# Where sixteen or seventeen pieces of context work stand among the expert products of a routed mixture

## The chip, the core and the metric

The kernel runs on one core of a Trainium2 chip. The metric is the device time of one execution in microseconds (us), lower is better. All data are fp32.

## What is computed

The reference is two residual blocks over 256 tokens of width 1024 (`x`), with 256 context tokens beside them (`ctx`). The part that matters here is the end of the first block and the start of the second:

```python
def hier_moe(h, wg, bg, we, be, w_gate, w_up, w_down):      # 4 groups of 8 experts, width 512
    p_group = softmax(t @ wg + bg);      g_idx = top 1 of 4 groups
    e_logits = (t @ we + be) of that group;  e_idx = top 2 of its 8 experts
    for gi in range(N_GROUPS):
        hid = silu(t @ w_gate[gi]) * (t @ w_up[gi]) * combine[:, gi]
        out = out + hid @ w_down[gi]

def second_block(x, c, ctx, ...):        # layer 0
    hc = rmsnorm(ctx, g_pre) * (1 + scale_c) + shift_c
    uc = hc @ w_in                        # q, k, v, gates, o, z, pool input and gate
    ... convolution, chunkwise mLSTM of 4 heads, head norm, multiscale pool, @ w_out
    ctx = ctx + gate_c * rmsnorm(yc, g_post)
```

The experts work on `x`, the second block's context side works on `ctx` alone, so the two are independent of each other. The kernel runs them in one stage.

## The kernel before, in words

The program is a list of stages. Each stage has one function for PE, one for ACT and one for DVE, and the engines meet at its end (`stage_end`). The stage of this case is the **expert stage**, `moe_pe`, `moe_act`, `moe_dve` and `moe_sync` (about 523 to 1167 us of the span). If no expert got too many tokens, it takes the sparse path: `sparse_pe`, `sparse_act`, `sparse_dve`, `sparse_sync`.

**The expert side.** The 32 experts are taken in 10 passes (`PASSES`): six passes of four experts, then four passes of two. Before a pass `gather(p)` (L2333) picks the tokens of the experts of that pass with one-hot products, and ACT and DVE copy them from two banks to `gath` (L2394, L2431). A pass has six **steps**, numbered 0 to 59 over all passes: two for the gate weights and two for the up weights (`project`, L2347), two for the down weights (`down`, L2364). Behind the fourth step stand the gather of the next pass, then four transposes of the hidden rows (L2380), which need DVE's product (L2453). A step of a four-expert pass reads four half-slots of 1 MB of weights, one of a two-expert pass reads two. There are 8 half-slots. SP issues the loads in order (L2219), and the load for half-slot number `at` waits until the step that used number `at - 8` has signalled `step_used`. So in a four-expert pass the weights of step n+2 are asked for when step n ends, and at most two steps of weights are on their way or waiting. In a two-expert pass it is four steps.

**The context side.** `body_pe`, `body_act` and `body_dve` are Python generators that emit the context work of the second block in 116 **pieces**, in a fixed order, with the same numbers on the three engines:

| pieces | work on PE | length on PE |
|---|---|---|
| 1 to 8 | keys and values of heads 0, 1 (L1418, L1433) | long, 3.5 us |
| 9 | gate columns (L1446, L1452) | 2.6 us |
| 10 to 27 | mLSTM heads 0 and 1: each one opening piece (L1463 to L1475), then eight small ones (L1486, L1491, L1497) | small, 0.7 to 2.7 us |
| 28 to 35 | output and gate rows (L1433) | long |
| 36 | transposes of the heads (L1506) | 1.2 us |
| 37 to 48 | queries, keys, values of heads 2, 3 | long |
| 49 to 66 | mLSTM heads 2 and 3 | small |
| 67 to 74, 75 | output and gate rows, transposes | long, 1.2 us |
| 76 to 83, 84 | pool input (L1418), an empty piece | long, 0 |
| 85 to 88 | pool products (L1522), each needs DVE's pool mean (L1900 to L1905), which needs the table `pool_inv` from DRAM | 2.0 us |
| 89 to 96 | pool gate (L1418) | long |
| 97 to 112 | output product (L1533, L1538) | long, 3.6 us |
| 113 to 116 | two norms | small, in a chain with ACT and DVE |

The context weights come through four slots of 1 MB that ACT loads (L1380), two of them when a projection has been taken from its banks. The pool tables are asked for at piece 79.

**How they are mixed.** `fill(body, p, i)` emits some pieces at the place i of pass p: places 0, 1, 2 behind the first three steps, 3 behind the fourth step and the gather, 4 behind the transposes, 5 behind the fifth step, 6, 7 and 8 behind the sixth, ahead of the first step of the next pass. In a four-expert pass the numbers are `FILL_FOUR`, in a two-expert pass `FILL_TWO`. `start(body)` emits four pieces between the first gather and the first pass, `finish(body)` emits what is left behind the last pass. ACT and DVE call the same functions at the same places of their own order, so that no engine waits for a piece that another one has not yet come to. On DVE `row_ids_dve` (L2301 to L2314, 16 small instructions) stands in pass 0 between the places 3 and 4. Behind `finish` ACT scales and DVE adds the experts' rows (L2426, L2477), which GpSimd has fetched back from DRAM (L2322).

Of the kernel before, what the change touches and what calls it, by code (L numbers as in the profile page):

```python
# [227 lines left out]
def build(nc, d, out):  # L228
    ctx = ExitStack()
    with ctx:  # L230
# [1989 lines left out]

        step_of = [n for n in range(6 * NPASS) for _ in range(PASSES[n // 6][1])]

        FILL_FOUR, FILL_TWO = (2, 2, 2, 2, 2, 2, 2, 1, 1), (0, 0, 0, 1, 0, 1, 0, 0, 0)

        def fill(body, p, i):

            for _ in range((FILL_FOUR if PASSES[p][1] == 4 else FILL_TWO)[i]):
                next(body, None)

        def start(body):  # L2230

            for _ in range(4):
                next(body, None)

        def finish(body):
# [89 lines left out]
        def sparse_pe(pe, body):  # L2325
            def gather(p):

                pe.wait_ge(pick_ready, p + 1)
                if p >= 2:
                    pe.wait_ge(py_out, 2 * p - 2)  # L2330
                for k in range(DT):
                    for t in range(TT):
                        mm = nc.tensor.matmul(bank[2 + k // 4][:, (k % 4) * P:(k % 4 + 1) * P], hrows[:, t, k * P:(k + 1) * P], pick[:, t, :],  # L2333
                                              start=(t == 0), stop=(t == 1), skip_group_check=True)
                    if k % 4 == 3:
                        mm.then_inc(gath_mm, 1)

            def project(p, b, n, at):

                experts = PASSES[p][1]  # L2340
                w = P // experts
                for half in range(2):
                    pe.wait_ge(step_in[(n + half) % 4], filled_to[n + half])
                    for k in range(4 * half, 4 * half + 4):
                        for e in range(experts):
                            rows = slice(e * w, (e + 1) * w)
                            mm = nc.tensor.matmul(bank[b][rows, :], gath[:, k, rows], half_slot[(load_at[n + half] + e) % NHALF][:, (k % 4) * 512:(k % 4 + 1) * 512],  # L2347
                                                  start=(k == 0), stop=(k == DT - 1), skip_group_check=True)
                    mm.then_inc(step_used, 1)
                    if at + half < 3:  # L2350
                        fill(body, p, at + half)
# [15 lines left out]
                    fill(body, p, 5 + half)  # L2367

            gather(0)
            start(body)  # L2370
            for p in range(NPASS):
                pe.wait_ge(gath_out, 2 * p + 2)
                project(p, 0, 6 * p, 0)
# [17 lines left out]
        def sparse_act(act, body):  # L2391
            def take_gathered(p):
                act.wait_ge(gath_mm, 2 * p + 1)
                nc.scalar.copy(gath[:, 0:4, :].rearrange("p k s -> p (k s)"), bank[2][:]).then_inc(gath_out, 1)  # L2394

            take_gathered(0)
            start(body)
            for p in range(NPASS):
                fill(body, p, 0)
                act.wait_ge(step_used, 6 * p + 2)  # L2400
# [27 lines left out]
        def sparse_dve(dve, body, chain):  # L2428
# [10 lines left out]
            def make_pick(p):  # L2439
                o, shape, first, experts, w = slots(p, pick)  # L2440
                nc.vector.tensor_tensor(o, bc(slot_no[:, 0:w].unsqueeze(1).unsqueeze(1), shape), bc(place[:, :, first:first + experts].unsqueeze(3), shape),  # L2441
                                        ALU.is_equal).then_inc(pick_ready, 1)

            make_pick(0)
            take_gathered(0)
            make_pick(1)
            start(body)
            for p in range(NPASS):
                for i in (0, 1, 2):
                    fill(body, p, i)  # L2450
# [790 lines left out]
```

## Time and profile before

| | |
|---|---|
| median of 3 runs | 1720.27 us (1718.19 to 1720.31) |
| the profiled execution | 1717.13 us, its span 1715.3 us |
| mean granted TensorE clock over the span | 0.944 |
| PE busy, DMA | 91% of the span; 397.57 MB, mean 232 GB/s |
| expert weights | 192 loads of 1 MB (SP), in three groups of 64 |
| context weights in this stage | 28 + 8 loads of 1 MB and the pool tables (ACT) |

PE is the matmul engine, PEld its weight loads, SPq and ACTq the queues that issue DMAs. The idle time in square brackets of a row is that of the engine just before the row, with what released it. A matmul in fp32 shows as two records.

### The profile page before, as it was taken

What the parts mean: (1) busy time and instruction counts of PE and PEld (TensorE: products, weight loads), DVE (VectorE), ACT (ScalarE), POOL (GpSimd) and SP (SyncE); (2) the same over time, 40 slices, a digit from 0 to 9 for tenths busy, and PEclk for the clock granted to TensorE, in tenths of its full rate; (3) what the DMA queues carried; (4) which work ended last, traced back from release to release, by engine and by line L of the source; (5) the groups of instructions that cost most, each with busy time, mean ns of one, the idle gap of its engine ahead of it and who ended that gap; (6) DMA issues with size and microseconds to landing.
All of it is one profiled execution on the core that took longest, in us unless ns stands there. A gap on an engine that the chain in (4) does not pass through costs nothing.

```text
span 1715.3 us, 22008 instructions
## 1 busy us (share of the span) xinstructions
PE 1555.3 (91%) x9293; PEld 1068.3 (62%) x9293; DVE 491.7 (29%) x1234; ACT 338.7 (20%) x698; POOL 4.1 (0%) x8
## 2 busy tenths in 40 slices
PE   6999988899979879997998999987889989999997
PEld 3655678778866434543365754456675775888666
DVE  2200064461234321222113100027343232022481
ACT  2310150112021112011210000014112132021461
POOL 0000000000000000000000000000000000000000
PEclk8999996699979889999999999997999999999998
DMA  9989530122138998999999999961313223323100
GB/s 375 421 353 371 202 144 1 48 99 103 49 152 341 376 414 361 407 392 418 418 404 410 408 414 408 367 255 40 146 49 147 104 93 139 134 82 147 49 2 25
DMA packets 54303, 397.57 MB, mean 232 GB/s; under 512 B 6359, under 2 KB 13688, under 8 KB 16440
## 3 DMA queue, kind: packets, MB, share of 16 engines
q1 hardware_dynamic: 40384, 341.85, 49.7%
q10 hardware_dynamic: 13240, 52.16, 7.7%
q0 software_dynamic: 576, 2.10, 0.4%
q8 instruction: 75, 1.23, 0.3%
q14 instruction: 28, 0.23, 0.0%
HBM read 389.80 MB, written 6.29 MB: 231 GB/s over the span
## 4 chain that ended last, share of the span: by engine, by line
PE 77%; DMA 10%; DVE 5%; ACT 4%; issue 2%; SPq 1%; PEld 1%; ACTq 1%; PEldq 0%; DVEq 0%
PE bank L681 15%; PE bank L1418 11%; PE bank L1433 8%; PE bank L2347 6%; DMA work<-in_moe_w_up 5%; PE bank L2364 4%; PE bank L1533 3%; PE bank L1538 3%; PE bank L526 3%; DMA work<-in_moe_w_gate 2%; PE bank L2333 2%; PE bank L712 2%; PE bank L1141 2%; PE bank L1129 2%; PE bank L870 2%
## 5 line engine op out<-in xcount | busy, mean ns | idle before, releaser
L681 PE MATMUL bank<-H,ring 128*128 128x256 f32 (+1 forms) x960 | 244.3, 413 | 6.1 <-ACT work L1058 4.0
L681 PEld LDWEIGHTS bank<-H,ring 128*128 128x128 f32 x960 | 182.7, 192 | 59.5 <-issue 34.2
L2347 PE MATMUL bank<-ring,work 128*32 128x512 f32 (+1 forms) x768 | 137.2, 626 | 15.0 <-DMA work<-in_moe_w_gate 6.2
L1418 PE MATMUL bank<-H,work 128*128 128x256 f32 x512 | 115.8, 385 | 0.4 <-issue 0.4
L1418 PE MATMUL bank<-H,ring 128*128 128x256 f32 x512 | 112.8, 380 | 0.0
L1418 PEld LDWEIGHTS bank<-H,work 128*128 128x128 f32 x512 | 97.2, 192 | 19.4 <-issue 6.4
L1418 PEld LDWEIGHTS bank<-H,ring 128*128 128x128 f32 x512 | 98.0, 192 | 13.6
L2347 PEld LDWEIGHTS bank<-ring,work 128*32 128x32 f32 (+1 forms) x768 | 36.4, 121 | 102.3 <-issue 82.9
L1433 PE MATMUL bank<-work,H 128*128 128x512 f32 x192 | 85.2, 596 | 0.0
L1433 PE MATMUL bank<-ring,H 128*128 128x512 f32 x192 | 83.0, 592 | 0.0
L2364 PE MATMUL bank<-ring,work 128*32 128x512 f32 (+1 forms) x384 | 67.3, 616 | 4.0 <-issue 2.2
L2347 PE MATMUL bank<-work 128*32 128x512 f32 (+1 forms) x256 | 65.5, 659 | 3.5 <-DMA work<-in_moe_w_up 3.5
L1433 PEld LDWEIGHTS bank<-work,H 128*128 128x128 f32 x192 | 35.7, 190 | 47.0 <-issue 46.9
L1433 PEld LDWEIGHTS bank<-ring,H 128*128 128x128 f32 x192 | 36.5, 190 | 44.2 <-issue 44.0
L526 PEld LDWEIGHTS bank<-work,csil 128*32 128x32 f32 x1536 | 42.5, 114 | 12.3 <-issue 11.0
L526 PE MATMUL bank<-work,csil 128*32 128x128 f32 x1536 | 49.5, 284 | 0.0
L2364 PEld LDWEIGHTS bank<-ring,work 128*32 128x32 f32 (+1 forms) x384 | 18.0, 120 | 44.4 <-issue 41.9
L2333 PEld LDWEIGHTS bank<-work 128*128 128x128 f32 x320 | 36.5, 192 | 11.2 <-issue 7.7
L2333 PE MATMUL bank<-work 128*128 128x128 f32 x320 | 38.4, 278 | 3.0 <-DVE work L2441 3.0
L1486 PE MATMUL bank<-work 128*128 128x257 f32 x64 | 22.2, 430 | 18.6 <-DVE work L1800 12.8
L1497 PE MATMUL bank<-work 128*128 128x257 f32 x96 | 29.4, 415 | 9.8 <-DVEq L1817 7.7
L2470 DVE COPY work<-bank 128x512 f32<-128x512 f32 x10 | 6.9, 691 | 107.5 <-PE bank L2364 107.5
(425 smaller groups left out, 1989.3 us busy)
## 6 DMA issues: line engine op xcount, KB each, us to landing
ring<-in_moe_w_gate SPq DMA_DIRECT2D x48, 1024.0 KB, 10.8
ring<-in_moe_w_up SPq DMA_DIRECT2D x48, 1024.0 KB, 9.0
ring<-in_moe_w_down SPq DMA_DIRECT2D x48, 1024.0 KB, 12.1
work<-in_ab_w_in ACTq DMA_DIRECT2D x28, 1024.0 KB, 10.3
ring<-in_ab_w_in SPq DMA_DIRECT2D x14, 2048.0 KB, 7.5
work<-in_ada_w SPq DMA_DIRECT2D x12, 2048.0 KB, 15.4
ring<-in_w_in SPq DMA_DIRECT2D x12, 2048.0 KB, 9.7
work<-in_w_mod SPq DMA_DIRECT2D x12, 2048.0 KB, 9.0
```

The lines of the kernel that those rows point to most:

```text
L526: mm = nc.tensor.matmul(bank[5][32 * g:32 * g + 32, 0:P], csil[:, m // 12, k, :], slot_k(mod_chunk[m], k, g * P, (g + 1) * P), start=(k == ...
L681: mm = nc.tensor.matmul(bank[i % NB][:, 0:n], weight(c, k, j * P, (j + 1) * P), rhs(k), start=(k == 0), stop=(k == kt - 1))
L712: mm = nc.tensor.matmul(bank[i % NB][:], H[:, k, t * P:(t + 1) * P], slot_k(c, k, 0, 512), start=(k == 0), stop=(k == DT - 1))
L870: mm = nc.tensor.matmul(bank[6 + h // 2][:, c0:c0 + CHUNK], st_all[:, i % 2, dr, h, :], cum[:, 0, dr, h, cidx * CHUNK:(cidx + 1) * CHUNK], ...
L1129: mm = nc.tensor.matmul(bank[4 + j % 2][:, half * T:(half + 1) * T], slot_w(c, k, j * P, (j + 1) * P), y[:, k, :], start=(k == 0), stop=(k ...
L1418: mm = nc.tensor.matmul(b[:, j * T:(j + 1) * T], w_k(m, n, k, at, at + P), H[:, k, m.s], start=(k == 0), stop=(k == DT - 1), skip_group_ch ...
L1433: mm = nc.tensor.matmul(b[:], H[:, k, at:at + P], w_k(m, n, k, 0, 512), start=(k == 0), stop=(k == DT - 1))
L1533: nc.tensor.matmul(b[:, j * T:(j + 1) * T], w_q(m, OUT[r], 8 + k, j * P, (j + 1) * P), m.yp[:, k, :], start=(j + k == 0), stop=False, skip ...
L1538: mm = nc.tensor.matmul(b[:, j * T:(j + 1) * T], w_q(m, OUT[r], k, j * P, (j + 1) * P), m.ym[:, k, :], start=False, stop=(k == 7), skip_gr ...
L2333: mm = nc.tensor.matmul(bank[2 + k // 4][:, (k % 4) * P:(k % 4 + 1) * P], hrows[:, t, k * P:(k + 1) * P], pick[:, t, :], start=(t == 0), s ...
L2347: mm = nc.tensor.matmul(bank[b][rows, :], gath[:, k, rows], half_slot[(load_at[n + half] + e) % NHALF][:, (k % 4) * 512:(k % 4 + 1) * 512] ...
L2364: mm = nc.tensor.matmul(bank[2 + side][rows, :], phid_t[:, f, rows], half_slot[(load_at[n + half] + e) % NHALF][:, at:at + 512], start=(f ...
```

## The change

The four pieces of `start` are no longer emitted, on any of the three engines, and `FILL_FOUR` goes from (2, 2, 2, 2, 2, 2, 2, 1, 1) to (1, 2, 2, 2, 2, 2, 2, 2, 2): 17 pieces a pass instead of 16, one fewer behind the first step, one more at each of the places 7 and 8. `FILL_TWO`, the order of the pieces and everything else stay.

```diff
-        FILL_FOUR, FILL_TWO = (2, 2, 2, 2, 2, 2, 2, 1, 1), (0, 0, 0, 1, 0, 1, 0, 0, 0)
+        FILL_FOUR, FILL_TWO = (1, 2, 2, 2, 2, 2, 2, 2, 2), (0, 0, 0, 1, 0, 1, 0, 0, 0)
...
-        def start(body):
-
-            for _ in range(4):
-                next(body, None)
-
...
             gather(0)
-            start(body)
             for p in range(NPASS):
...
             take_gathered(0)
-            start(body)
             for p in range(NPASS):
...
             make_pick(0)
             take_gathered(0)
             make_pick(1)
-            start(body)
             for p in range(NPASS):
```

Pieces emitted when a pass begins:

| ahead of | step | before | after |
|---|---|---|---|
| pass 0 | 0 | 4 | 0 |
| pass 1 | 6 | 20 | 17 |
| pass 2 | 12 | 36 | 34 |
| pass 3 | 18 | 52 | 51 |
| pass 4 | 24 | 68 | 68 |
| pass 5 | 30 | 84 | 85 |
| pass 6 | 36 | 100 | 102 |
| `finish` | | 108 | 110 |

## Rows read from the trace of the kernel before

**Rows 1.** Stretches: length, busy us per engine, PEclk, DMA share, GB/s
```profile
523.30:832.60 309.30, 274.71 (x1504) 142.87 (x1504) 88.72 (x244) 52.54 (x98) 0.00 (x0) 0.94 0.95 387
832.60:995.30 162.70, 153.50 (x865) 96.35 (x864) 31.48 (x49) 17.45 (x32) 0.00 (x0) 0.98 1.00 409
```

**Rows 2.** Timeline of PE, first gather to first steps: start, us, what
```profile
523.29 3.84 PE L2333 MATMUL bank<-work 128*128 128x128 f32 x32 [3.05 <-DVE work L2441]
526.97 13.98 PE L1418 MATMUL bank<-H,work 128*128 128x256 f32 x64
540.87 3.64 PE L2347 MATMUL bank<-ring,work 128*32 128x512 f32 x32
```

**Rows 3.** Timeline of SP's queue: the first expert loads
```profile
507.77 3.78 SPq L2219 DMA_DIRECT2D ring<-in_moe_w_gate  x6
544.58 11.45 SPq L2219 DMA_DIRECT2D ring<-in_moe_w_up  x6
```

**Rows 4.** Stretches as in rows 1: where the DMA engines were partly idle
```profile
533.80:542.50 8.70, 8.70 (x50) 6.49 (x52) 7.92 (x24) 1.17 (x2) 0.00 (x0) 1.00 0.18 43
...
585.00:605.00 20.00, 15.05 (x86) 6.14 (x86) 8.22 (x31) 1.53 (x3) 0.00 (x0) 0.83 0.82 329
657.50:665.50 8.00, 8.00 (x43) 2.75 (x42) 0.05 (x1) 0.00 (x0) 0.00 (x0) 1.00 0.32 105
```

**Rows 5.** Timeline of PE: waits and checkpoints of steps 4 to 24
```profile
588.50 1.23 PE L1497 MATMUL bank<-work 128*128 128x257 f32 x2 [4.03 <-DVEq L1817]
589.65 5.41 PE L2364 MATMUL bank<-ring,work 128*32 128x512 f32 x32
...
640.54 0.62 PE L2347 MATMUL bank<-ring,work 128*32 128x512 f32 x2 [1.72 <-DMA work<-in_moe_w_up]
...
688.01 1.22 PE L1506 MATMUL bank<-ident,work 128*128 128x128 f32 x8 [3.75 <-DVE work L1865]
689.16 5.15 PE L2347 MATMUL bank<-ring,work 128*32 128x512 f32 x32
...
767.91 3.64 PE L2347 MATMUL bank<-ring,work 128*32 128x512 f32 x32
...
798.58 0.62 PE L2347 MATMUL bank<-ring,work 128*32 128x512 f32 x2 [2.42 <-DMA work<-in_moe_w_up]
...
832.65 3.64 PE L2347 MATMUL bank<-ring,work 128*32 128x512 f32 x32
```

**Rows 6.** PE's waits from 540 to 641 us: total, times, longest
```profile
PE bank L2347 <- DMA work<-in_moe_w_up: 2.3, 2, 1.7
PE bank L2347 <- DMA work<-in_moe_w_gate: 2.0, 1, 2.0
PE bank L2347 <- DMA ring<-in_moe_w_up: 2.0, 1, 2.0
PE bank L1486 <- issue: 1.7, 1, 1.7
```

**Rows 7.** Timeline, all engines, around the pool pieces
```profile
892.18 0.70 ACTq L1380 DMA_DIRECT2D work<-in_pool_inv  x1
...
916.41 1.30 DVE L1900 TENSOR_TENSOR_SCAN work<-work 128x548 f32<-128x548 f32 x1 [16.90 <-DMA work<-in_pool_inv]
...
919.99 5.85 PE L1522 MATMUL bank<-work 128*128 128x256 f32 x16 [7.12 <-issue]
```

**Rows 8.** Timeline of PE: DMA waits of steps 27 and 51
```profile
865.42 0.62 PE L2347 MATMUL bank<-ring,work 128*32 128x512 f32 x2 [0.79 <-DMA work<-in_moe_w_up]
...
1075.45 6.58 PE L2347 MATMUL bank<-work 128*64 128x512 f32 x16 [3.54 <-DMA work<-in_moe_w_up]
```

**Rows 9.** Timeline, all engines: behind the last pass
```profile
1130.64 7.20 PE L1533 MATMUL bank<-work 128*128 128x256 f32 x32
...
1144.73 0.93 POOL L2322 DMA_INDIRECT work<-expert_rows,work  x1 [0.30 <-issue]
...
1163.07 2.17 ACT L2426 ACTIVATE work<-work 128x1024 f32<-128x1024 f32 x2
```

## The prediction, made before the change was run

> **What bounds the kernel now.** I read first the long stretches of the expert stage [rows 1]. PE is busy for 274.7 of 309.3 us up to step 24, and the DMA share is 0.95 there and 1.00 in the 162.7 us behind it. So both run near their limit, and neither is it throughout. The list of PE's waits says where the weights come last: up to step 9 PE waits for them 2.3 + 2.0 + 2.0 = 6.3 us in four waits [rows 6], and 2.42 us at step 21 [rows 5]. They stand where the pieces between the steps are small, those of the mLSTM heads. Where they are long it is the other way round: PE runs without a gap and the DMA engines run dry, with a share of 0.32 from 657.5 to 665.5 us [rows 4], because the next weights are asked for only when a step ends. The change has to be judged by what it does to these two kinds of gap.
>
> The place itself: the gather ends at 527.1, four long pieces follow, step 0 starts at 540.87 [rows 2]. The first eight loads left at 507.77, the next ones only at 544.58, when step 0 had ended [rows 3]. From 533.8 to 542.5 the DMA share is 0.18 [rows 4]: 8.7 x 0.82 = 7.1 us of DMA time are lost. PE loses nothing, its four pieces are work that has to be done.
>
> **The rule of the sum.** Steps and pieces are the same in both kernels. Behind the last pass a chain of PE, ACT and DVE runs from the last piece to 1163.07, and GpSimd's last fetch went out at 1144.73, 18 us ahead of ACT's scaling of the rows [rows 9]; two pieces fewer in `finish` (2 x 3.6 = 7.2 us) leave that fetch covered. So the two extra pieces in the passes cost what `finish` saves, and the change is worth exactly what it does to PE's idle time and to the slow clock behind it. Checkpoints are the start of step 24, where both kernels have emitted 68 pieces, and the start of step 36 (100 and 102 pieces).
>
> **Stretch one, to step 24.** Edit by edit:
> 1. The first product. The last of the two copies of the gather takes about 0.7 us (my estimate from the size of the gap, 523.29 + 3.84 = 527.13 against a start not before 528). Cost: 1 us of idle PE that `start` covered. The weights of step 0 are no wait: at the 409 GB/s of a share of 1.00 [rows 1] its 4.2 MB take 10 us from 507.8, so they are there by about 519.
> 2. The 7.1 us of DMA time are won: step 0 ends at 531.7 and its successor's loads go out then, while the first eight are still landing.
> 3. `row_ids_dve` no longer meets a small piece. In the kernel before PE waits 4.03 us for DVE behind it and the next step takes 5.41 instead of 3.64 us [rows 5, 2], 5.8 us in all. After the change the pieces at that place are 8 and 9, a long one and the gate columns. The DMA engines lost 20 x 0.18 = 3.6 us in that stretch [rows 4], which goes with it.
> 4. So the weights of step 9, which PE waits for at 640.54 [rows 5], can be there at 640.5 - 7.1 - 3.6 = 629.8. Is PE there by then? From 540.87 to 640.54 are 99.7 us. Take off the 6.3 us of DMA waits [rows 6], 3.4 us of slow clock behind two of them (1.7 each, my estimate from 5.41 against 3.64 us [rows 5, 2]) and the 5.8 us of point 3: 84.2 us with pieces 5 to 26. The new kernel has pieces 1 to 22: plus 14.0 [rows 2], minus 5.9 for pieces 23 to 26 (my estimate: two gaps of 2.9 us between steps), plus 2.7 for openings of a head that now stand right ahead of its next piece twice (such a wait is 1.7 us [rows 6]). That is 95.0 us from 528.0, thus 623.0. The weights are the later: step 9 at 629.8, 10.7 us sooner, of which 5.9 us are pieces not yet done.
> 5. Steps 9 to 18 take 767.91 - 640.54 = 127.4 us now [rows 5]. New: +5.9 (pieces 23 to 26), -0.7 (piece 52 is behind step 18), -5.3 (the transposes, piece 36, waited 3.75 us behind piece 35, and the step behind them took 5.15 us [rows 5]; now a step stands between), -0.6 (a wait for weights). Against that a new wait at step 14: steps 12 and 13 have pieces 35 and 36, 37 between, 15.4 us from the start of step 12 to step 14, while its weights go out at the end of step 12 and need 3.6 + 1.5 to restart + 10.0 + 1.0, and up to 5.0 more beside the context load that piece 35 releases: 16.1 to 21.1. I take 4.5 us and 2.5 us of slow clock. The long wait of point 4 costs 2.8 us of slow clock too. Sum 136.5, step 18 at 766.3.
> 6. Steps 18 to 24 take 64.7 us now, step 21 being 30.7 us behind step 18 [rows 5]. New: the weights set steps 20 and 21: 3.6 + 1.5 + 20.0 + 1.0 = 26.1 us. Then 34.1 as now, + 3.8 (pieces 57, 58) + 1.5 (an opening) - 1.2 (a wait) = 38.2. Together 64.3, step 24 at 830.6.
>
> **Stretch one gives -2 us**; from -8 (no wait at step 14, weights of step 9 sooner) to +2.
>
> The kernel's rows bear on one rule: behind the 3.75 us wait the step takes 5.15 us and not 3.64 [rows 5, 2]; PE was idle before it, and the clock fell to its lower level of 1.2 GHz for part of it. The Trainium skill, TensorE: Matmul & The Clock Gate, section HAM oscillation, says that a wait for a DMA can be paid for twice in this way and that every such wait does it anew. By that rule more waits, as I expect behind step 24, are dearer than their idle time; the two slow products [rows 5] agree.
>
> **Stretch two, steps 24 to 36.** Here I expect a loss, since six pieces instead of four stand between a pass's last step and the next pass's first, and the pool pieces move ahead of step 30.
> - Step 27: one piece fewer behind step 24 and a context load beside its weights: a wait of 2.5 + 1.7 of clock instead of 0.79 us [rows 8]. +3.4.
> - Piece 75 now stands right behind piece 74, as 36 stood behind 35: +5.3.
> - The pool. Its tables are asked for at 892.18 and used by DVE at 916.41, 24 us later, and PE starts at 919.99 after 7.12 us of idle time, and two pool pieces take 5.85 instead of 4.0 us [rows 7]: 9.0 us. The request comes 7 us later relative to step 28, but fewer expert weights are ahead of it: 6.1 + 1.6 MB from there, 18 us. PE reaches piece 85 16 us behind the request (step 29, four pieces), waits 5.2 us, and that ahead of step 30: -2.3 with 1.5 us of slow clock.
> - Step 32: while PE stood ahead of step 30 nothing asked for its weights. They come 3.6 + 1.5 + 10 + 1 us behind the start of step 30 and PE is there 13.5 us behind it or sooner: 3.5 us and 2.5 us of clock. +6.
> - Steps 30 and 36: the six long pieces behind step 35 leave the DMA engines dry for longer (21.3 us against 10 us of weights), which costs PE nothing since the four steps behind it have their weights.
>
> Sum +12.4. The two DMA waits are the least certain, since either falls away if the engines are 3 us sooner. I take **+8**, from +4 to +13.
>
> That the pool tables take 24 us is a row [rows 7]. Behind it, by a rule of the Trainium skill, DMA: Bandwidth & Descriptors, section Queues, rings and completion order, an engine takes turns between the queues it has work for, packet by packet. By it a table in small packets lands when the experts' queue runs dry; the trace agrees, and by it the wait would be 5 us as above and not 12.
>
> **Stretch three, steps 36 to the end.** The one DMA wait is 3.54 us at step 51, and the product takes 6.58 and not 3.6 us [rows 8], 6.5 us in all. The weights for steps 40 to 51 and the output weights of pieces 100 and 104 have to come in the 76.5 us that PE needs (995.4 to 1075.45 less the wait). The loads of piece 104 leave a pass and a half sooner after the change, and those of piece 100 are in before step 36 ends: 25.2 + 2.1 + 1.1 MB, 69.4 us at 409 GB/s and 4.5 us to start, 74 us. No wait is left, with 2.6 us to spare. I take **-5**, from -6.5 to 0.
>
> **Sum.** -2 + 8 - 5 = +1 us. The profiled execution of 1717.1 us becomes 1718.1. The median of the runs is 3.2 us above that execution, so the forecast is **1721.3 us**. A measurement of this kernel can tell about 0.2%, 3.4 us, from no change; the forecast is no change.
>
> **Rivals.**
> - *Faster*: the stage hangs on the DMA engines throughout, and every us of their time is worth one. Then the 7.1 us of the first hole and the 3.6 us behind `row_ids_dve` come back whole: -10.7, or 1709.6 us. For it speaks the share of 0.95 to 1.00 [rows 1] and that PE waits for weights again right behind such holes. Against it: holes of 5 us open [rows 4] and PE does not feel them. Half of this gain, with stretch two at its low end, is 1715.
> - *Slower*: the six pieces. A four-expert step asks for 10 us of weights, six long pieces and a step last 24.9 us. From the point where the DMA engines have less than 15 us of work queued, each pass boundary with long pieces opens a hole 7 us larger than before; behind it the next short gap makes PE wait, with the clock on top. With stretch two at 12.4, one at 0 and a wait left at step 51 it is +12, 1732; with half of that, 1727.
> - *It does not do what it says*: the first product could stand and wait for weights. By the loads' own times they are in by 519 us, at the slowest by 534 when all eight have landed [rows 3, 4]. Then steps 0 and 1 start 6 us later, the first hole is still shorter, and the time is 1720.
>
> **Chances.** No change as forecast 0.34, the third rival 0.03, faster 0.27, slower 0.36 (its two sizes share it). The forecast is the likeliest single case by a small margin over either size of the slower one. Faster by over 0.2% 0.27, within 0.37, slower 0.36. The range holds the sum of the stretches' ends less the corners, -10 to +10: 1711 to 1731. The forecast case alone is 1717 to 1724.
>
> **What would show it.** Step 0 at 528 and the next loads at 531.7; no wait behind `row_ids_dve`; step 9 near 630; step 24 within a few us of 830.6; DMA waits at steps 14, 20, 27 and 32; a wait of some 4 us at piece 75; piece 85 with about 5 us of idle time ahead of step 30; step 36 some 13 us later than now (7 of it the two pieces), and step 51 without a wait. If step 24 starts at 825 or sooner, the DMA engines were worth more than I give them; if step 36 is over 18 us late, the six pieces cost more.

## The result: 22 us slower

The changed kernel takes 1742.51 us (median of 4 runs, 1737.1 to 1746.21), the kernel before beside it 1720.29 us: ratio 1.0122, interval 1.0096 to 1.0148. The forecast was 1721.3 us with a range to 1731, so both missed. The profiled execution took 1742.09 us with a span of 1740.3 us, 25.0 us more than before, at a mean granted clock of 0.936 (0.944 before). From here on lines are those of each kernel's own file: L2342 and L2359 of the changed kernel are the products of L2347 and L2364 before, L2328 the gather of L2333.

Windows of the changed kernel, the three stretches of the prediction (columns: busy us and instructions of each engine, granted clock, DMA share, GB/s). They answer to [rows 1]:

```profile
520.00:841.70 321.70, 278.92 (x1506) 144.48 (x1507) 88.95 (x244) 53.56 (x99) 0.00 (x0) 0.93 0.93 379
841.70:1025.60 183.90, 164.55 (x899) 102.81 (x898) 31.81 (x49) 21.23 (x36) 0.00 (x0) 0.95 0.91 370
1025.60:1186.30 160.70, 142.50 (x801) 75.37 (x800) 19.73 (x43) 22.55 (x42) 3.98 (x4) 0.95 0.87 344
```

The DMA share fell in the first two (0.95 and 1.00 before): the 7 us of DMA time that the change wins at the start are lost again further on. Against the prediction, each stretch counted from the start of the gather (523.29 before, 519.95 after: the stage itself began 3.3 us sooner):

| stretch | before | after | difference, less the pieces moved | predicted |
|---|---|---|---|---|
| gather to step 24 | 309.4 us | 321.7 us | +12.4 | -2 |
| step 24 to 36 | 162.7 | 183.9 | +21.2 - 7.2 = +14.0 | +8 |
| step 36 to ACT L1687 | 149.5 | 140.4 | -9.1 + 7.2 = -1.9 | -5 |

Then the whole mixing part of the stage as one window, from the gather to the end of PE's products of the two norms, first before, then after; both hold the same 3,200 products:

```profile
523.30:1159.30 636.00, 579.37 (x3200) 321.14 (x3200) 135.73 (x327) 88.28 (x164) 3.88 (x4) 0.95 0.94 385
```
```profile
520.00:1180.40 660.40, 585.95 (x3200) 322.65 (x3200) 136.32 (x327) 92.03 (x167) 3.98 (x4) 0.94 0.92 372
```

So 24.4 us are 6.6 us of busy time (same products, slower clock) and 17.8 us of idle time. What the idle time was for stands in PE's waits, summed from 520 to 1190 us (in all, times, longest). Before:

```profile
PE bank L2347 <- DMA work<-in_moe_w_up: 9.7, 6, 3.5
PE bank L1497 <- DVEq L1817: 7.7, 8, 4.0
PE bank L2347 <- DMA work<-in_moe_w_gate: 6.2, 2, 4.3
PE bank L2347 <- DMA ring<-in_moe_w_up: 2.6, 2, 2.0
PE bank L1486 <- DVEq L1841: 2.3, 8, 0.4
PE bank L1486 <- DVE work L1800: 2.2, 1, 2.2
PE bank L1486 <- issue: 1.7, 1, 1.7
PE bank L2364 <- DMA work<-in_moe_w_down: 1.1, 1, 1.1
```

After:

```profile
PE bank L2342 <- DMA ring<-in_moe_w_up: 21.3, 5, 6.4
PE bank L1486 <- DVE work L1800: 9.0, 4, 3.0
PE bank L2342 <- DMA work<-in_moe_w_up: 7.3, 3, 4.0
PE bank L1486 <- DVEq L1841: 5.6, 9, 1.3
PE bank L1446 <- ACT work L1594: 4.0, 1, 4.0
PE bank L2342 <- DMA work<-in_moe_w_gate: 2.3, 2, 1.3
PE bank L1497 <- DVEq L1817: 2.0, 4, 0.7
```

Weights: 19.6 us before, 30.9 after, +11.3. The small pieces of the heads (L1486): 6.2 and 14.6, +8.4. The gate columns (L1446): 0.4 and 4.0, +3.6. The row numbers, which show at L1497: -5.7. That is 17.6 of the 17.8 us. Of the 6.6 us of busy time 1.6 are the gather at the start (5.47 against 3.84 us), which varies from run to run; see the last part.

Where they stand (PE's timeline of the changed kernel; in brackets the idle time just before and its releaser):

```profile
519.95 5.47 PE L2328 MATMUL bank<-work 128*128 128x128 f32 x32 [3.04 <-DVE work L2434]
526.20 3.64 PE L2342 MATMUL bank<-ring,work 128*32 128x512 f32 x32 [0.78 <-DVE work L2424]
...
577.95 1.00 PE L1446 MATMUL bank<-ident,work 64*128 64x64 f32 x8 [3.97 <-ACT work L1594]
578.75 3.52 PE L1452 MATMUL bank<-work,ident 64*128 64x2 f32 x16
582.19 4.99 PE L2359 MATMUL bank<-ring,work 128*32 128x512 f32 x32
...
589.16 0.60 PE L1475 MATMUL bank<-ident,work 128*128 128x128 f32 x4
591.92 1.20 PE L1486 MATMUL bank<-work 128*128 128x257 f32 x2 [2.16 <-DVE work L1800]
...
705.92 6.26 PE L2342 MATMUL bank<-ring,work 128*32 128x512 f32 x32 [6.04 <-DMA ring<-in_moe_w_up]
...
791.80 1.08 PE L2342 MATMUL bank<-ring,work 128*32 128x512 f32 x4 [6.37 <-DMA ring<-in_moe_w_up]
...
874.21 0.62 PE L2342 MATMUL bank<-ring,work 128*32 128x512 f32 x2 [3.98 <-DMA work<-in_moe_w_up]
...
934.46 3.75 PE L1522 MATMUL bank<-work 128*128 128x256 f32 x8 [7.26 <-issue]
...
956.04 5.34 PE L2342 MATMUL bank<-ring,work 128*32 128x512 f32 x32 [4.23 <-DMA ring<-in_moe_w_up]
```

These are the gather and step 0; piece 9, the gate columns, and step 4 behind it; the end of opening 10 and piece 11; and the steps 14, 20, 27 and 32 with the first pool piece between. The rows of the steps 20 and 27 hold only their first instructions; the whole steps took 5.99 and 5.34 us.

### The profile page after: what moved, and what is told of

The parts are those of the page before. It is cut to its first block, busy times and chain, and to the rows that moved or that the text cites. A ratio compares the mean times of both kernels' runs of the same rounds, so it can differ in the third digit from the quotient of the medians.

```text
span 1740.3 us, 22011 instructions
## 1 busy us (share of the span) xinstructions
PE 1565.2 (90%) x9293; PEld 1072.7 (62%) x9293; DVE 492.2 (28%) x1234; ACT 342.6 (20%) x701; POOL 4.2 (0%) x8
## 4 chain that ended last, share of the span: by engine, by line
PE 77%; DMA 9%; DVE 5%; ACT 4%; issue 2%; SPq 1%; PEld 1%; ACTq 0%; PEldq 0%; DVEq 0%
PE bank L681 15%; PE bank L1418 11%; PE bank L1433 9%; PE bank L2342 7%; PE bank L2359 4%; PE bank L1533 3%; PE bank L1538 3%; DMA work<-in_moe_w_up 3%; PE bank L526 3%; DMA ring<-in_moe_w_up 2%; DMA work<-in_moe_w_gate 2%; PE bank L2328 2%; PE bank L712 2%; PE bank L1141 2%; PE bank L1129 2%
## 5 line engine op out<-in xcount | busy, mean ns | idle before, releaser
L2342 PE MATMUL bank<-ring,work 128*32 128x512 f32 (+1 forms) x768 | 145.8, 672 | 31.6 <-DMA ring<-in_moe_w_up 21.3
L2342 PEld LDWEIGHTS bank<-ring,work 128*32 128x32 f32 (+1 forms) x768 | 37.8, 129 | 127.0 <-issue 89.4
L2359 PE MATMUL bank<-ring,work 128*32 128x512 f32 (+1 forms) x384 | 67.9, 617 | 2.8 <-issue 2.2
L2342 PE MATMUL bank<-work 128*32 128x512 f32 (+1 forms) x256 | 61.3, 624 | 0.0
L1486 PE MATMUL bank<-work 128*128 128x257 f32 x64 | 22.9, 443 | 27.0 <-DVE work L1800 19.7
L2328 PEld LDWEIGHTS bank<-work 128*128 128x128 f32 x320 | 38.1, 199 | 11.5 <-issue 8.0
L2359 PEld LDWEIGHTS bank<-ring,work 128*32 128x32 f32 (+1 forms) x384 | 18.1, 120 | 42.5 <-issue 41.6
L2328 PE MATMUL bank<-work 128*128 128x128 f32 x320 | 40.0, 285 | 3.0 <-DVE work L2434 3.0
L2445 DVE TENSOR_TENSOR work<-work,bank 128x512 f32<-128x512 f32 x10 | 6.9, 689 | 113.5 <-PE bank L2342 113.5
L546 DVE TENSOR_TENSOR mod<-bank,vecs 128x8 f32<-128x8 f32 x24 | 4.0, 167 | 106.7 <-PE bank L537 106.7
## 6 DMA issues: line engine op xcount, KB each, us to landing
work<-in_ada_w SPq DMA_DIRECT2D x12, 2048.0 KB, 15.6
```

The costliest lines, as they stand in the source:

```text
L2359: mm = nc.tensor.matmul(bank[2 + side][rows, :], phid_t[:, f, rows], half_slot[(load_at[n + half] + e) % NHALF][:, at:at + 512], start=(f ...
```

## The experiments

Each run's ratio is to the kernel before on the same chip. The runs were made on several chips, on which the kernel before had medians of 1717.2 to 1720.3 us, so a difference in us between two runs of different groups can be off by some 3 us.

### One piece behind the first step

The theories of these first four runs: PLACE, the second piece behind each first step; START, the four pieces of `start`; GAP, the six pieces at the pass boundary; GATE, the wait of the gate columns.

```diff
-        FILL_FOUR = (1, 2, 2, 2, 2, 2, 2, 2, 2)
+        FILL_FOUR = (2, 2, 2, 2, 2, 2, 2, 2, 1)
```

> The change with FILL_FOUR (2,2,2,2,2,2,2,2,1) in the place of (1,2,2,2,2,2,2,2,2): no start, 17 pieces a pass, but two behind the first step and one at place 8. PLACE theory (the loss comes from the one piece taken from behind the first step and put behind the last: the weights of the third step are asked for when the first ends, and too little work stands between the two): waits of PE at steps 14, 20 and 32 (6.0, 6.4, 4.2 us after the change) shrink to 2.5 us or less each, and the time is 8 to 18 us below that of the change, 1725 to 1735. START theory (the loss comes from taking start away, by which the gate columns and the head pieces meet other steps): within 4 us of the change, 1738 to 1746. GAP theory (six pieces in a row behind the last step leave the DMA engines dry, and each us of that is lost): five in a row instead of six, a sixth of the loss, about 1738.

Measured 1728.21 us, ratio 1.0043 (1.002 to 1.0065): 14.3 us of the 22 come back. There is no wait at step 14 any more, that at step 20 is 4.60 instead of 6.37 us, and PE's DMA waits sum to 18.0 instead of 30.9 us. The time is in PLACE's range; the wait at step 20 is not the 2.5 us or less that it asked for. Openings right ahead of their next piece wait twice and not four times (5.1 and 9.0 us). The piece is also taken out of the six at the pass boundary, so this run alone doesn't part PLACE from GAP.

The same move alone, in the kernel before with its start kept:

```diff
-        FILL_FOUR = (2, 2, 2, 2, 2, 2, 2, 1, 1)
+        FILL_FOUR = (1, 2, 2, 2, 2, 2, 2, 2, 1)
```

> The kernel before with FILL_FOUR (1,2,2,2,2,2,2,2,1): start stays, 16 pieces a pass as before, one piece alone moved from behind the first step to place 7. PLACE theory: most of the loss of 22 us comes with this, 1733 to 1745, with waits of 4 us and more at the third step of passes. START theory: no start is taken away, so within 4 us of before, 1716 to 1724. GAP theory: five pieces in a row instead of four, 3 to 8 us lost, 1723 to 1728.

Measured 1752.41 us, ratio 1.0166 (1.0135 to 1.0196): 32 us by the medians, 28 by the ratio, for one piece a pass. That is more than the whole change and more than any of the three theories said. The profile is of its slowest execution, 1757.82 us. Its waits of PE:

```profile
PE bank L2347 <- DMA work<-in_moe_w_up: 9.9, 4, 4.2
PE bank L2347 <- DMA ring<-in_moe_w_up: 9.5, 4, 4.2
PE bank L1486 <- DVE work L1800: 9.2, 4, 3.1
PE bank L1506 <- DVE work L1865: 7.5, 2, 3.8
PE bank L1486 <- DVEq L1841: 6.0, 6, 4.1
```

The weights are only 24.7 us of it. What nearly every other row shows is that the pieces have changed partners: all four openings (10, 19, 49, 58) now stand right ahead of their next piece, both transposes of heads (36, 75, L1506) right behind the product that they need, and the gate columns wait 4.0 us. So a moved piece does two things: it moves the asking for weights, and it shifts the pieces behind it against the steps by one.

### The start alone, and the gate columns alone

```diff
-        FILL_FOUR = (1, 2, 2, 2, 2, 2, 2, 2, 2)
+        FILL_FOUR = (2, 2, 2, 2, 2, 2, 2, 1, 1)
```

> The change with FILL_FOUR as before, (2,2,2,2,2,2,2,1,1): start is gone, 16 pieces a pass, four more pieces in finish. PLACE theory: small, 1718 to 1730, what is lost here is the wait of the gate columns of 4.0 us with its slow clock and the gap of the DMA engines behind it. START theory: the whole loss, 1738 to 1746. My theory of the prediction (first gap of the DMA engines won back): 1712 to 1720.

Measured 1731.93 us, ratio 1.0059 (1.0038 to 1.0079): the start taken away alone costs 12 us, between the ranges of PLACE and START and outside both. The DMA waits are 33.6 us, the longest 7.62 us, and the gate columns wait 4.0 us.

```diff
+        FILL_ZERO = (1, 2, 2, 2, 1, 3, 2, 2, 2)
```

This list is for pass 0 alone; the other passes stay as the change has them.

> The change with, in pass 0 alone, (1,2,2,2,1,3,2,2,2): piece 9, the gate columns, stands behind step 4 instead of ahead of it; all other passes as in the change. GATE theory (the wait of 3.97 us for ACT's exponentials ahead of step 4 holds back the release of the weight slots and costs more than itself): the wait and the slow product of step 4 (4.99 us) go, step 4 starts some 8 us sooner, the DMA share of 575 to 590 rises from 0.61 to over 0.9, and 4 to 9 us are won of the change, 1733 to 1739. PLACE theory alone: the 4 us are taken up by the next wait for weights, steps 7 to 9, and it is within 3 us of the change.

Measured 1731.61 us, ratio 1.0059 (1.0042 to 1.0076), 10.9 us less than the change, for a wait of 3.97 us; GATE had said 4 to 9. The timeline says how:

```profile
573.47 3.64 PE L2360 MATMUL bank<-ring,work 128*32 128x512 f32 x32
577.51 0.71 PE L1446 MATMUL bank<-ident,work 64*128 64x64 f32 x8 [0.40 <-ACT work L1594]
578.06 1.89 PE L1452 MATMUL bank<-work,ident 64*128 64x2 f32 x16
```

Against the rows of the changed kernel above, the wait is 3.6 us shorter, the same two groups of products take 1.9 us less and step 4 3.64 instead of 4.99 us. That is 6.9 us, 3.3 of them clock: the two groups ran at a granted clock of 0.53 (577.9 to 582.2 us) and here at 1.00 (577.5 to 580.0). The rule that the prediction cited (the Trainium skill, TensorE: Matmul & The Clock Gate, section HAM oscillation) is told there for waits for a DMA; the trace shows the same behind a wait for ScalarE. In the changed kernel no step could end meanwhile and let weights be asked for, and the DMA share fell to 0.61 from 575 to 590 us, with a granted clock of 0.77:

```profile
530.00:575.00 45.00, 42.97 (x228) 24.47 (x227) 20.12 (x60) 4.05 (x8) 0.00 (x0) 1.00 1.01 420
575.00:590.00 15.00, 11.81 (x72) 7.40 (x72) 1.29 (x6) 3.77 (x10) 0.00 (x0) 0.77 0.61 236
```

The first of these rows shows what the change was good for, 45 us without a hole behind step 0; the second loses 15 x 0.39 = 5.9 us of it. With the gate columns moved the share of 575 to 590 us is 1.01.

Over the same part of the stage as above this run takes 649.2 us and the change 660.4:

```profile
521.10:1170.30 649.20, 579.32 (x3200) 319.89 (x3200) 136.27 (x328) 92.15 (x167) 4.12 (x4) 0.95 0.93 377
```

Of these 11.2 us 6.6 are busy time (579.3 against 585.95 us; 1.6 of them the gather, 3.84 here) and 4.6 idle time. PE's waits for weights stay at 30.0 us (30.9). So PE came 4 us sooner to the later steps and waited there no longer: the weights came sooner by as much. All of the gain lies up to step 24, which stands 310.7 us behind the start of the gather, against 321.7 in the change and 309.4 in the kernel before; steps 24 to 36 take 183.9 us in both.

The cause of the wait is on ACT: it copies the banks of piece 8 at 574.87, loads a table, and its exponentials end at 577.9; PE was through with piece 8 at 573.98.

```profile
574.87 0.59 ACT L1578 COPY work<-bank 128x512 f32<-128x512 f32 x1 [3.71 <-PE bank L1433]
575.48 1.28 ACT L1593 ACT_TABLE_LOAD   x1
576.77 1.03 ACT L1593 ACTIVATE work<-work 64x256 f32<-64x256 f32 x3
577.71 0.19 ACT L1594 ACTIVATE work<-work 64x2 f32<-64x2 f32 x1
```

Both repairs in one kernel:

```diff
+        FILL_ZERO = (1, 2, 2, 2, 1, 3, 2, 2, 2)
-        FILL_FOUR = (1, 2, 2, 2, 2, 2, 2, 2, 2)
+        FILL_FOUR = (2, 2, 2, 2, 2, 2, 2, 2, 1)
```

> The changed kernel with both repairs: (2,2,2,2,2,2,2,2,1) in all four-expert passes, as in the first run of the study, except pass 0, where the gate columns follow step 4 as in the fourth. If the two causes are apart (14.3 us for the place of a piece, 10.9 us for the gate columns) it is 1717 us, that is the time of the kernel before. If each only takes away the same lateness of the weights, it stays at 1726 to 1731, where each of them alone was.

Measured 1720.45 us, ratio 1.0024 (1.001 to 1.0038). The two add up in the main: 22.1 of 25.2 us by the medians, but 17 of 24 by the ratios, since the kernel before was 3 us faster on this chip. The time lies between the two that were expected. So a kernel without `start` is again about where the kernel before was (0.1 to 0.4% slower), although its first hole in the DMA work is gone.

### Weights or engines: half the bytes

```diff
-        sp.dma_start(half_slot[at % NHALF], half_src(w, e[i], half))
+        cols = slice(0, HALF if n < 2 else HALF // 2)
+        sp.dma_start(half_slot[at % NHALF][:, cols], half_src(w, e[i], half)[:, cols])
```

> The kernel before, in which each expert load behind the first eight brings only the first half of its columns (the products read what stood there; the number of loads, their order, all waits and all products stay). WEIGHTS (the loss of the change is made of waits for expert weights and of the slow clock behind them): the 19.6 us of DMA waits in the stage all but go, with some 8 us of slow clock: 1688 to 1698 us. ENGINES (the loss is made of waits of TensorE for ScalarE and VectorE): also faster by its DMA waits, the same time; the two theories part in the difference to the next kernel.

> The changed kernel with the same halved loads. WEIGHTS: its 30.9 us of DMA waits go as well, and what is left against the kernel before with halved loads is the 4.0 us of the gate columns with their slow clock, less the wait behind the row numbers: the difference between the two is 0 to 5 us, not 22. ENGINES: the difference stays, 15 us or more, since no wait for ScalarE or VectorE depends on the bytes.

These kernels leave out half of the bytes of each expert load behind the first eight; the products, 3,200 in the stage, are as many. Measured 1682.27 and 1699.52 us (ratios 0.9807, 0.9781 to 0.9832, and 0.9892, 0.9856 to 0.9928). The first is 6 us below the range that was expected (1688 to 1698). The difference is 17.2 us, 15 by the ratios, where WEIGHTS had said 0 to 5 and ENGINES 15 or more: WEIGHTS, my theory at that point, falls. In the kernel before PE then has no DMA wait at all, in the changed one 4.4 us. What is left of the changed kernel's waits:

```profile
PE bank L1486 <- DVE work L1800: 9.1, 4, 3.0
PE bank L1486 <- DVEq L1841: 5.6, 9, 1.3
PE bank L1506 <- DVE work L1865: 4.3, 2, 3.9
PE bank L1446 <- ACT work L1594: 4.0, 1, 4.0
PE bank L2343 <- DMA ring<-in_moe_w_up: 3.3, 3, 2.6
PE bank L1497 <- DVEq L1817: 2.0, 4, 0.7
```

But for the row of the weights they are the same rows as with whole loads, to 0.1 us. The windows from the gather on, before and after:

```profile
520.40:1119.30 598.90, 568.35 (x3200) 319.91 (x3200) 135.75 (x327) 88.37 (x164) 3.90 (x4) 0.97 0.70 249
```
```profile
523.00:1137.40 614.40, 573.77 (x3200) 320.76 (x3200) 136.36 (x328) 92.03 (x167) 4.00 (x4) 0.97 0.68 241
```

15.5 us: 5.4 of clock, 4.4 of DMA waits, the rest engines (+8.5 at L1486, +3.4 at L1446, -5.8 at L1497). So the loss has an engine side that no weight explains, and I had put nearly none of it into the sum.

The checkpoints say where it is, with the 7.2 us of the two pieces taken off as above. Up to step 24 the change costs 9.6 us with half loads (298.8 against 289.3) and 12.4 with whole ones, or 11.2 and 10.8 when the gather counts as 3.84 us in all four; from step 24 to 36 it costs 4.5 us (164.0 against 152.3, less 7.2) and 14.0 with whole ones. So the loss up to step 24 is mostly there without late weights, and that of steps 24 to 36 mostly is not.

### The same wait taken away, with whole and with half loads

```diff
+        FILLS = ((1, 2, 2, 2, 1, 2, 2, 2, 4), (1, 2, 2, 2, 2, 2, 2, 2, 1), the others as the change has them)
```

> The changed kernel, with pass 0 dealt (1,2,2,2,1,2,2,2,4) and pass 1 (1,2,2,2,2,2,2,2,1); everything from piece 35 on stands where the change has it. So the gate columns follow step 4, and neither of the openings 10 and 19 stands right ahead of its own next piece any more. PAIRS (what the halved loads left, about 15 us, is made of pieces put right behind the piece on whose way through ScalarE and VectorE they wait: gate columns 4.0 us, openings 2.1 to 3.0 us each, each with 1.6 us of slow clock behind it): it beats the run that moved the gate columns alone (1731.6 us) by two openings, some 7 us, less what the weights take back: 1723 to 1728. DISTANCE (only the weights' lookahead counts and the gate columns were a chance gain): within 2 us of 1731.6.

Measured 1732.69 us, ratio 1.007 (1.0048 to 1.0091), no better than moving the gate columns alone (1731.61). PAIRS missed, DISTANCE hit. The two waits of the openings did go, and the weights took their place:

```profile
603.92 3.64 PE L2353 MATMUL bank<-ring,work 128*32 128x512 f32 x32
...
620.87 5.14 PE L2353 MATMUL bank<-ring,work 128*32 128x512 f32 x32 [5.25 <-DMA ring<-in_moe_w_up]
```

This is step 6, and step 8 with a wait of 5.25 us for weights, where the run that moved the gate columns alone had 1.40 us. Over the stage the waits at L1486 fell from 14.2 to 9.5 us and those for weights rose from 30.0 to 33.8. They were asked for at the end of step 6 (607.5) and PE could start on them 13.3 us later, and no opening saved in between can change that. That pass 0 had one piece more ahead of step 6 made the asking 2.2 us later as well.

> The kernel of the run before (gate columns behind step 4, openings 10 and 19 apart from their next pieces), with each expert load behind the first eight bringing only the first half of its columns. COVER (a wait of TensorE for an engine is worth its length with slow clock only where the weights are not later): against the changed kernel with halved loads (1699.5 us) the gate columns' 4.0 us, two openings of 2.2 us and some 3 us of slow clock come off: 1686 to 1690 us. MOVED (the waits turn up elsewhere on the engines): 1694 us or more.

Measured 1683.12 us, ratio 0.9801 (0.9781 to 0.9821), 3 us below COVER's range and 11 below MOVED's. It is 16.4 us less than the changed kernel with half loads, and level with the kernel before with half loads. So without late weights, the new lists of passes 0 and 1, which put three pieces apart from their forerunners (9, 11 and 20), are worth all that the change costs there; with whole loads the same lists gave 9.8 us. That it is the three pairs and not the other pieces that moved with them is not shown: PE's idle time in the stage fell by 6.4 us and its busy time by 6.9 (566.8 against 573.8).

```diff
-                if p == 0:
+                if p == 2:
                     row_ids_dve(dve, chain)
```

> The kernel before with the sixteen VectorE instructions of the row numbers moved from pass 0 to the same place of pass 2, where long pieces stand. The prediction took 5.8 us of TensorE time and 3.6 us of DMA time from their wait of 4.03 us. If the wait is worth what the prediction gave it, 1711 to 1715 us; if the weights behind it are the later in any case, and set steps 8 and 9, only 0 to 3 us of it come back: 1716 to 1720.

Measured 1716.83 us, ratio 0.9989 (0.9975 to 1.0003): 2.1 us, and not to be told from nothing. The wait of 4.03 us [rows 5] is gone, and there are new ones for weights: 2.35 us at step 5 and 4.94 at step 8. In all, the waits for weights rise from 19.6 to 22.6 us.

> The kernel before with the row numbers in pass 2 and halved loads. With whole loads this gave 2 us. COVER: here nothing stands behind the wait of 4.0 us, so it comes back with its slow clock: 4 to 6 us against 1682.3 us, 1676 to 1678. MOVED: 0 to 2 us, 1680 to 1682.

Measured 1677.17 us, ratio 0.9762 (0.9746 to 0.9778): 5.1 us less than without the move, as COVER said. So the one wait was worth 2 us with whole loads and 5.1 us with half loads. Both have the sign of COVER; that the two differ is within the spread of the four medians.

> The changed kernel dealt (2,2,2,2,2,2,2,2,1), as in the first run of the study, with halved loads. With whole loads this one moved piece gave 14.3 us. COVER: it gave them through the weights of the third steps (DMA waits 30.9 to 17.9 us) and through one opening fewer; here only the opening counts: 1693 to 1698 us. ENGINES: it acts through the engines' waits: 1685 to 1690 us.

Measured 1687.08 us, ratio 0.9824 (0.9807 to 0.984): 12.4 us less than the changed kernel with half loads. ENGINES hit and COVER missed: I had put the 14.3 us of this piece down to the weights of the third steps, and most of it is there without them. By its windows 8.5 us are clock (busy 565.27 against 573.77 us) and 5.5 us waits at L1486. But the profile is of its fastest execution (1681.11 us, clock 0.956, the other three 0.945 to 0.947), so part of the 8.5 us is chance. What the weights add to it with whole loads is at most a few us, within the spread of these runs.

### Other lists

> The kernel before, its start kept, with the seventeen pieces of a four-expert pass dealt (3,3,2,1,1,3,2,1,0) instead of (2,2,2,2,2,2,2,1,1). LOOKAHEAD (a piece is worth most as cover where the weights asked for last are needed next, and costs most where none of a step's slots comes free for long, that is behind gather and transposes): the boundary has 1 + 0 + 3 pieces less one, the middle has 2 and not 4: 1708 to 1718 us. SHIFT (any move away from the old places costs as much as the one moved piece of the earlier run did): 1730 us or more.

(The list holds sixteen pieces, as before, not seventeen.) Measured 1715.64 us, ratio 0.9987 (0.9966 to 1.0007): in the expected range, and not to be told from no change.

```diff
+        FILLS = ((2, 2, 2, 2, 0, 2, 2, 2, 3), (2, 2, 2, 2, 2, 2, 2, 2, 2), (3, 3, 2, 2, 1, 3, 2, 2, 0),
+                 (2, 3, 2, 2, 1, 3, 2, 2, 0), (2, 2, 2, 2, 1, 3, 2, 2, 1), (2, 2, 2, 2, 1, 3, 2, 2, 1), FILL_TWO four times)
```

> No pieces ahead of step 0, as in the changed kernel, and a list for each four-expert pass: (2,2,2,2,0,2,2,2,3), (2,2,2,2,2,2,2,2,2), (3,3,2,2,1,3,2,2,0), (2,3,2,2,1,3,2,2,0), and twice (2,2,2,2,1,3,2,2,1). By these a step stands between 8 and 9, 10 and 11, 19 and 20, 35 and 36, 49 and 50, 58 and 59, 74 and 75, and two or three pieces stand behind each first step. PAIRS AND LOOKAHEAD together: no wait of TensorE for VectorE at an opening and none ahead of the transposes of the heads, DMA waits below 15 us: 1700 to 1710 us, faster than the kernel before. If the start is worth its 7 us of DMA time only on paper: 1716 to 1722.

Measured 1709.1 us, ratio 0.995 (0.9925 to 0.9974). Without `start`, as in the change, the kernel is faster than before by 9.8 us with these lists, which put the pairs apart and two or three pieces behind each first step; which of the two did it, this run alone does not say. The transposes wait 0.4 us and no piece waits for the opening ahead of it (no row at L1486 with the releaser L1800); DMA waits are 17.5 us, above the 15 expected.

> The kernel before with its start of four pieces kept, and lists for every pass that put few pieces behind the gather where the weights run short and many where they stand ready: (2,2,2,3,2,2,2,1,2), (2,3,2,0,1,2,2,1,0), (4,2,3,0,1,3,3,0,1), (0,4,2,3,1,1,1,2,2), (1,2,3,1,2,2,3,0,2), (2,3,1,4,0,2,1,1,0), and in the two-expert passes (0,1,0,1,1,0,0,1,1), (0,0,0,0,0,1,0,0,1), (0,0,0,0,1,0,1,0,0), (0,0,0,0,1,0,0,0,0). LOOKAHEAD: 1700 to 1712 us, with the start's hole in the DMA share still there, so that the start is no fault by itself. If it is, it stays at 1716 or above.

Measured 1707.48 us, ratio 0.9924 (0.9901 to 0.9947): the start is no fault in itself.

> The kernel before, start kept, another set of lists: (2,2,2,3,0,4,3,0,0), (1,3,3,0,1,2,2,1,2), (2,2,2,0,2,2,1,0,4), (4,3,2,0,4,3,2,0,2), (0,3,1,0,3,3,1,3,1), (2,2,1,3,1,1,0,1,2), and in the two-expert passes (1,1,0,0,0,0,2,0,0), (0,0,0,0,0,0,0,0,1), (1,0,0,1,0,0,0,1,0), (1,0,0,0,1,0,0,0,0). COVER: engine waits may stand where weights are late anyway, and the weights are asked for evenly: 1700 to 1708 us. If the two lists tried are already as good as the DMA engines allow: 1707 us or more.

Measured 1702.38 us, ratio 0.9904 (0.9887 to 0.9921), the best median of all whole-load kernels, 15.6 us below the kernel before; from the run ahead of it (0.9901 to 0.9947) it can't be told. Its window over the stage, from its slowest execution (1710.1 us):

```profile
523.10:1148.20 625.10, 573.01 (x3200) 319.47 (x3200) 135.90 (x327) 88.36 (x164) 3.89 (x4) 0.97 0.96 392
```

It keeps three openings ahead of their next pieces (7.2 us of waits) and has 16.6 us of DMA waits. It gains in the busy time (573.01 against 579.37 us before) and in the DMA share: 0.96 against 0.94. An estimate from these rows: the stage moves 385 GB/s x 636.0 us = 245 MB; at the 420 GB/s of the full stretch above that is 583 us, and PE's products take 579 us at the clock they had. They are two loads of nearly one size, and every order tried with whole loads pays 42 us (625 us, this run) to 88 us (671 us, the piece moved with the start kept) for their not lying on each other.

## Why the prediction was wrong

The prediction had +1 us and the stage lost 24.4. The 23.4 us between them fall on four places: 8.5 up to step 9, 5.9 from there to step 24, 6.0 from step 24 to 36, and 3.1 behind it (each rounded).

**Step 0 and the first hole (points 1 and 2): right, but for the slower gather.** PE waited 0.78 us (1 predicted), step 0 ended at 529.8, and the next loads left at once:

```profile
529.90 9.11 SPq L2219 DMA_DIRECT2D ring<-in_moe_w_up  x6
```

The gather took 5.47 and not 3.84 us. It took about one or the other in every kernel profiled here, 5.46 for instance in the kernel before with half loads.

**Point 3, the step that failed.** It took 5.8 us of PE and 3.6 us of DMA time from a wait behind `row_ids_dve`, because "the pieces at that place are 8 and 9, a long one and the gate columns". The wait did go. But I never asked what the gate columns wait for. Their releaser is ACT's exponentials behind piece 8's copy, a chain of 4 us from the end of piece 8, and in the change nothing lies between 8 and 9. Moving piece 9 behind step 4 gave 10.9 us. It also put step 9 at 105.6 us behind the start of the gather, where the prediction had 106.5. And the gain on the other side of this point was too large by itself: 5.8 us of PE time and 3.6 of DMA time were taken for the wait of 4.03 us, and taking it out of the kernel before gave 2 us, within the noise.

**Point 4** inherits it: step 9 stands 115.0 us behind the start of the gather, 106.5 predicted, 117.3 before [rows 2, 5]. The weights of a step were taken as hanging on the DMA engines' lost time. They hang as well on when the step two earlier ends, and a wait of PE ahead of that moves them too: the run that moved the gate columns alone lost 4 us of waits for engines and its waits for weights stayed at 30 us.

**Points 5 and 6: right in kind, too small.** Step 9 to 18: 138.5 us, 136.5 predicted. Step 14 waited 6.04 us with a product of 6.26 us, 4.5 + 2.5 predicted; the piece behind the opening waited 3.04 us at 771.23, which was not in it. Step 18 to 24: 68.2 us, 64.3 predicted; step 20 waited 6.37 us, and was reached 13.4 us behind the end of step 18. Together with point 4 (8.5 us) these make the 14.4 us between -2 and +12.4: 8.5 + 2.0 + 3.9.

**Openings.** "Plus 2.7 for openings of a head" was the only term for them in point 4, 1.5 in point 6. It took 1.7 us for such a wait; those of the changed kernel took 1.6 to 3.0 us, at four openings and not one. The waits at L1486 rose by 8.4 us. Which pieces share a place can be counted from the lists, and I had the lists.

**Stretch two, the second step that failed: the sum of the terms held, the choice did not.** Step 27 waited 3.98 us with a step of 5.34 (2.5 + 1.7), step 32 4.23 us (3.5). Piece 75 waited 3.75 us, but the 5.3 us had slow clock behind it, and none came: the next two long pieces took 7.07 us, as elsewhere. The pool waited 7.26 us (5.2), as its table took 20.8 us from request to use (18), and its first piece and step 30 ran slow, so that this term of -2.3 was about +1. The sum of my terms was 12.4 us and 14.0 came. I took +8, because "either falls away if the engines are 3 us sooner". Nothing in the rows said that they would be.

**Stretch three.** Step 51 had no wait, as predicted. But step 45 waited 2.58 us with a product of 5.35:

```profile
1071.69 0.65 PE L2342 MATMUL bank<-ring,work 128*64 128x512 f32 x2 [2.58 <-DMA ring<-in_moe_w_up]
```

That is 4.3 us with the slower product (3.60 elsewhere), more than the 3.1 us between -5 and -1.9.

**The rivals.** The slower one had the sign and the size nearest (1727 and 1732), though it was still 10 us short, by six pieces in a row. Its 12.4 us for stretch two nearly came (14.0), but its 0 for stretch one did not (12.4), and six pieces in a row are not what the runs show first: with the gate columns moved 10.9 us came back although the six pieces stayed, and the kernel without `start` and with its four pieces at the boundary as before was still 12 us slow. The lists of the latter shift other pieces too, so it does not price the six pieces by themselves. What stood in no case was that all pieces are shifted against the steps. The faster rival is refuted twice: the first hole was won and the time rose, and the row numbers' hole gave 2 us.

**What stays open.** How the 22 us divide between weights and engines has no single answer here. The changed kernel loses 17 us with half loads, and the rest, 5 us, is what weights add; with the intervals of both ratios it is anything from nothing to 15 us, and by the two pairs of profiled executions 8.9 (24.4 less 15.5), most of it in steps 24 to 36. But the gate columns' 10.9 and the moved piece's 14.3 us were measured with whole loads, and the slow clock, 6.6 us of the whole, follows both kinds of wait; no run here holds the clock and varies the rest. Nor was each opening taken by itself, and piece 75 and the pool pieces were in no run of their own.

## What to carry to other kernels

When work is dealt between fixed steps, write down for each piece what it waits for and how long that takes from the end of its forerunner; moving one piece shifts all behind it, and every such pair that loses the step between it is a new wait. Then take the two limits together. A wait of the engine can be worth more than its length, where it delays the asking for weights and slows the clock (4.0 us gave 10.9), and less where a wait for weights grows in its place (4.0 us gave 2, within the noise). An own sum of terms is not to be cut because it looks large.

## What had not been expected of the hardware

- Behind a wait of 3.97 us the next three groups of products took 3.3 us longer in all (1.00 + 3.52 + 4.99 against 0.71 + 1.89 + 3.64); the granted clock was 0.53 from 577.9 to 582.2 us. It was 0.53 too behind the 2.00 us wait for weights of step 7 in the kernel before (620.4 to 624.0), so here the slow clock followed a wait for another engine as it did one for a DMA.
- The busy time of the same products went, with whole loads, from 573 us (the second set of lists) to 593 us (one piece fewer behind the first step, start kept), a spread of 20 us that no list of idle times shows. Single executions add to such a spread; both profiles are of the slowest execution of their kernel.
- Half the bytes of the expert weights gave only 35 us in the kernel before, of 1717 on the same chip: the DMA engines at a share of 0.94 over the stage were nearly hidden.
- A four-expert step's weights were usable 13.3 and 13.4 us behind their asking with the queue empty (step 8 of the run that put the openings apart, step 20 of the changed kernel), 10 us of it transfer at the full rate. The prediction had 1.5 + 10.0 + 1.0 = 12.5 us for this. Ahead of step 20 the DMA share was 0.73 from 778.4 to 783.0 us, 1.2 us of restart; no row shows the last 1.0 us by itself.
